# One expert's rows transposed two experts ahead, and the next expert's first products put into the waits of the current one

## The reference, cut to what matters

```python
pg_top, g_sel = lax.top_k(pg, 1)              # one of 4 groups of experts
top_v, top_i = lax.top_k(le_sel, TOP_K)       # 2 of its 8 experts
expert_idx = g_sel * EXPERTS_PER_GROUP + top_i
...
def expert_block(args):
    xe, e = args
    return (jax.nn.silu(xe @ w_gate[e]) * (xe @ w_up[e])) @ w_down[e]
...
x = x + g2 * hier_moe(h, ...)
```

## Time and profile before

| | us |
|---|---|
| three runs: median, lowest, highest | 1513.91, 1513.27, 1514.66 |
| the profiled execution's own time | 1513.77 |
| its span, from the first instruction to the last | 1511.4 |
| PE busy | 1326.7 (88%) |
| DVE busy | 597.8 (40%) |
| ACT busy | 357.1 (24%) |
| POOL busy | 268.0 (18%) |
| mean granted clock of PE, as a share of full speed | 0.958 |

### The profile page before, as it was taken

One profiled execution on the slowest core, in us unless ns is written; L12 is line 12 of the kernel. 1 busy time (PEld: TensorE's weight loads), 2 busy tenths in 40 slices (PEclk: granted clock), 3 DMA queues, 4 the chain that ended last, 5 costly groups with the idle time before them and its releaser, 6 DMA issues.

```text
span 1511.4 us, 18434 instructions
## 1 busy us (share of the span) xinstructions
PE 1326.7 (88%) x6928; PEld 767.9 (51%) x6928; DVE 597.8 (40%) x1314; ACT 357.1 (24%) x791; POOL 268.0 (18%) x283
## 2 busy tenths in 40 slices
PE   5899899988998898888998999999889969997883
PEld 1446546655745554444444565566464545554441
DVE  5635522357716321433154251435782541221112
ACT  1411022545402111111202211244551211111111
POOL 0201200000100353322221030000010015333222
PEclk8999999999999799999987999999999979999997
DMA  8801220555494799999943112135307489999984
GB/s 288 318 16 56 101 84 12 215 191 180 133 361 166 293 327 379 410 404 404 358 170 118 56 58 70 58 133 202 112 1 297 160 299 387 400 400 403 402 343 147
DMA packets 100228, 336.83 MB, mean 223 GB/s; under 512 B 29988, under 2 KB 34724, under 8 KB 74890
## 3 DMA queue, kind: packets, MB, share of 16 engines
q1 hardware_dynamic: 74600, 305.52, 52.1%
q0 software_dynamic: 15072, 16.85, 5.0%
q10 hardware_dynamic: 10468, 13.28, 2.5%
HBM read 324.13 MB, written 29.00 MB: 234 GB/s over the span
## 4 chain that ended last, share of the span: by engine, by line
PE 77%; DVE 12%; ACT 4%; issue 4%; DMA 1%; POOL 1%; SPq 0%; DVEq 0%; POOLq 0%; ACTq 0%
PE bank L504 71%; PE bank L785 3%; PE bank L896 2%; DVE pr_r L2145 2%; ACT pr_r L1502 2%; DVE ht_r L2005 1%; DVE pr_r L2148 1%; PE bank L622 1%; DMA big<-in_ada_w_dram 1%; DVE mix_r L2019 1%; DVE big L1736 1%; DVE small L2003 0%; DMA x_tok<-x_rows 0%; DVE big L1923 0%; DVE ht_r L1989 0%
## 5 line engine op out<-in xcount | busy, mean ns | idle before, releaser
L504 PE MATMUL bank<-big,pr_r 128*64 128x256 f32 (+2 forms) x3032 | 426.3, 400 | 43.8 <-DVE pr_r L2148 22.6
L504 PEld LDWEIGHTS bank<-big,pr_r 128*64 128x64 f32 (+1 forms) x3032 | 258.3, 152 | 181.7 <-issue 93.6
L504 PE MATMUL bank<-big,ht_r 128*128 128x512 f32 (+3 forms) x832 | 309.1, 555 | 1.9 <-ACT ht_r L1455 1.9
L504 PEld LDWEIGHTS bank<-big,ht_r 128*128 128x128 f32 (+1 forms) x832 | 143.5, 189 | 133.0 <-issue 121.5
L504 PE MATMUL bank<-big 128*128 128x256 f32 (+4 forms) x496 | 169.4, 480 | 22.5 <-DVE big L1930 5.9
L1651 POOL DMA_INDIRECT x_rows<-ht_r,slot_i x64 | 102.0, 1594 | 321.4 <-DVE ht_r L2151 302.8
L504 PEld LDWEIGHTS bank<-big 128*128 128x128 f32 (+2 forms) x496 | 92.4, 198 | 67.2 <-issue 29.8
L1502 ACT ACTIVATE pr_r<-bank 64x256 f32<-64x256 f32 x64 | 24.1, 377 | 403.4 <-PE bank L504 403.4
L2145 DVE TENSOR_TENSOR pr_r<-pr_r,bank 64x256 f32<-64x256 f32 x65 | 27.5, 423 | 219.6 <-ACT pr_r L1502 214.6
L2151 DVE SCALAR_TENSOR_TENSOR ht_r<-bank,mix_r,mod 128x512 f32<-128x512 f32 x65 | 48.8, 751 | 132.6 <-PE bank L504 132.6
L504 PE MATMUL bank<-ht_r,big 128*128 128x512 f32 x192 | 85.4, 607 | 1.4 <-ACT ht_r L1341 1.4
(11 more groups left out here) (299 smaller groups left out, 1237.5 us busy)
## 6 DMA issues: line engine op xcount, KB each, us to landing
big<-in_moe_w_gate_dram SPq DMA_DIRECT2D x59, 1024.0 KB, 17.8
big<-in_moe_w_up_dram SPq DMA_DIRECT2D x59, 1024.0 KB, 22.3
big<-in_moe_w_down_dram SPq DMA_DIRECT2D x59, 1024.0 KB, 26.3
big<-in_ada_w_dram SPq DMA_DIRECT2D x16, 3072.0 KB, 11.3
big<-in_w_in_dram SPq DMA_DIRECT2D x4, 3072.0 KB, 13.6
big<-in_w_out_dram SPq DMA_DIRECT2D x4, 2048.0 KB, 9.3
mod<-in_ada_b_dram SPq DMA_DIRECT2D x12, 512.0 KB, 10.4
x_tok<-in_moe_w_gate_dram SPq DMA_DIRECT2D x6, 1024.0 KB, 17.0
```

The costliest lines, as they stand in the source:

```text
L504: return nc.tensor.matmul(o, l, r, start=start, stop=stop)
```

## The change

PE's order becomes, for expert e: gate and up of e, steps 2 to 7; the row transposes of e + 2 (`x_turn`); step 0 of gate and up of e + 1 (`begin`); the activation transposes of e; step 1 of gate and up of e + 1; down of e. The waits go with the work. `x_turn(e + 2)` waits for the gather of e + 2, and `begin(e + 1)` for the weights of e + 1. ACT's copies of the transposed rows follow the new order. The number of matmuls and of transfers is the same, and the programs of POOL, DVE and SP are not edited. There are still four row buffers.

```diff
-                def gate_up(b, s):
+                def gate_up(b, s, ks=range(KT)):
                     wg, wu, _ = expert_slot(s)
-                    for k in range(KT):
+                    for k in ks:
...
-                def expert(e):
-                    b, s = e % 2, EXPERT_SLOTS[l][e]
+                def x_turn(e):
+
+                    pe.wait_ge(gathered[e % 4], NE // 4 * 16 * l + 16 * (e // 4 + 1))
+                    if e >= 2:
+                        pe.wait_ge(xt_ready, NE * l + e - 1)
+                    pe.sem_inc(waited, 1)
+                    x_transpose(e % 2, e % 4).then_inc(xt_done, 1)
+
+                def begin(e):
+
+                    s = EXPERT_SLOTS[l][e]
                     pe.wait_ge(xt_ready, NE * l + e + 1)
                     pe.wait_ge(slot_full[s], expert_full(e, l))
                     if e >= 2:
                         pe.wait_ge(acth_ready, NE * l + e - 1)
-                    gate_up(b, s).then_inc(gu_done, 1)
+                    gate_up(e % 2, s, range(1))
+
+                def expert(e):
+                    b, s = e % 2, EXPERT_SLOTS[l][e]
+                    gate_up(b, s, range(2 if e else 1, KT)).then_inc(gu_done, 1)
                     if e == 0:
...
+                        x_turn(1)
+                    if e + 2 < NE:
+                        x_turn(e + 2)
                     if e + 1 < NE:
-                        pe.wait_ge(gathered[(e + 1) % 4], NE // 4 * 16 * l + 16 * ((e + 1) // 4 + 1))
-                        if e >= 1:
-                            pe.wait_ge(xt_ready, NE * l + e)
-                        pe.sem_inc(waited, 1)
-                        x_transpose(1 - b, (e + 1) % 4).then_inc(xt_done, 1)
+                        begin(e + 1)
                     pe.wait_ge(acth_ready, NE * l + e + 1)
...
                     act_transpose(b).then_inc(at_done, 1)
+                    if e + 1 < NE:
+                        gate_up(1 - b, EXPERT_SLOTS[l][e + 1], range(1, 2))
                     pe.wait_ge(actT_ready, NE * l + e + 1)
...
-                pe.wait_ge(gathered[0], NE // 4 * 16 * l + 16)
-                pe.sem_inc(waited, 1)
-                x_transpose(0, 0).then_inc(xt_done, 1)
+                x_turn(0)
+                begin(0)
                 for e in range(NE):
...
# ScalarE's program
-                    if e + 1 < NE:
-                        act.wait_ge(xt_done, NE * l + e + 2)
-                        x_evac(1 - b).then_inc(xt_ready, 1)
+                    for n in ((1, 2) if e == 0 else (e + 2,)):
+                        if n < NE:
+                            act.wait_ge(xt_done, NE * l + n + 1)
+                            x_evac(n % 2).then_inc(xt_ready, 1)
```

## The result

| | before | after |
|---|---|---|
| runs timed together: median (lowest to highest), us | 1513.59 (1512.09 to 1514.66) | 1566.93 (1563.49 to 1572.23) |
| the profiled execution's own time, us | 1513.77 | 1564.18 |
| its span, us | 1511.4 | 1561.8 |
| mean granted clock of PE | 0.958 | 0.933 |

The ratio is 1.0359, with a 95% interval from 1.0328 to 1.0389: 3.6% slower. Slower was forecast (+18.8 us), but the profiled execution lost 50.4 us, and the time lies outside the range.

The account below looks back on a forecast made before the run. PE's chain of one expert and the stream of weights were both taken as near their limit. Late gathers added 10.8 us in layer 1 and 8.0 in layer 0 to 1513.8: 1532.6 us, range 1520 to 1548.

Parts of the forecast that it names:

- The loop: From one expert's down through POOL's scatter, gather and row transposes to the down two experts later: 16.4 us.
- The free parts: Splitting gate and up costs PE nothing; ACT's changed order lies beside PE's work, else 0.6 us at expert 0.
- The prediction's own sign of being wrong: Wrong if gathers land under 5.5 us, PE waits for weights all through layer 1, or clock share falls well below 0.98.
- D(5) = 1268.5 + 8.8 + 2.1 = 1279.4. Twelve loops of 16.4 give D(29) = 1476.2: In layer 1, expert 5's down starts at 1279.4 us; twelve two-expert turns of 16.4 us bring expert 29's to 1476.2.
- Layer 0: In layer 0, later weight loads plus the moved wait for weights start expert 31's down at 775.1 us, +8.0 us.
- So this adds 5.8 us of dry time: In layer 0, expert 10's loads go out later, with DMA engines already run dry: 5.8 us more dry time.
- The bound of 9: In layer 0, upper bound in us, with slow gathers, on the shift lasting to the end; the lower was 2.
- So the shift stays: After expert 31's down in layer 0, PE goes on into its own long products, so the +8.0 us lasts.
- D: Rival: PE's clock falls in the new waits, 20 us more in layer 1, 1553 us; chance 0.09 in full.
- A: Rival: gathers land in time, under 5.5 us; 1514.5 us, no change; chance 0.06.
- B: Rival: the weight stream has slack too, PE's pace of 6.5 us per expert holds; about 1480 us; chance 0.02.
- C: Gathers near 7.5 us: layer 1 at weights' pace, +2.1; layer 0 +4 to +8; 1520 to 1524 us; chance 0.09.

Follow-up runs that it names:

- the first experiment: Changed kernel, but POOL issues the gather of e + 4 ahead of the scatter of e instead of behind it: 1519.88 us, 1.0054.
- twelve fillers: Changed kernel with twelve 128x128 identity transposes on PE ahead of each wait for a gather, from expert 4 on (layer 0: 4 to 13): 1546.14 us, 1.0198.
- the split: Down weights get their own semaphores, waited for at down: kernel before 1.0004; changed kernel 1.0387, or 1.0000 with the gather issued ahead of the scatter.
- the lighter stream: Changed kernel with half of layer 1's gate and up weights not loaded: 1529.58 us, 1.0093; the kernel before with the same: 1500.39 us, 0.9903.

## Why the prediction was wrong

*The loop was right.* The gather of two experts ahead ends PE's longest waits, the loop is the one described, and the two old waits all but vanish. The free parts were free: with the gather out of the way PE's own period was 6.55 us (the first experiment), 6.5 by forecast. The sum put the fall of the clock in the new waits at nothing, and left it to a rival. The time is off by the length of a turn and by how the turns start. The prediction's own sign of being wrong came true: the clock's share fell to 0.88 in the earlier trace rows's stretch of layer 1.

*The step that failed is "D(5) = 1268.5 + 8.8 + 2.1 = 1279.4. Twelve loops of 16.4 give D(29) = 1476.2".* It took every turn at the full clock and at the median gather of before. The changed kernel, mean of the ten turns from D(5) to D(25) of layer 1, 1297.8 to 1482.8 us, and beside it the same turns with twelve fillers (1294.9 to 1470.0 us; its landings are not in the trace, so its gather is the time from issue to PE's start less 0.13, and at most that, since in two of the ten turns PE came later):

| part of a turn, us | forecast | measured | with twelve fillers |
|---|---|---|---|
| down to the gather's issue | 5.5 | 5.95 | 5.65 |
| gather | 8.8 | 9.56 | 9.51 |
| to PE's start | 0.1 | 0.13 | 0.13 |
| row transposes to the next down | 2.0 | 2.86 | 2.22 |
| sum | 16.4 | 18.5 | 17.5 |

The turns without a fall have 5.5 in the first part and 2.1 in the fourth. So of 2.1 us too few, 1.3 are the clock and 0.8 the gather. The fillers take most of the clock's share away and leave the gather's. Why the gathers took 0.8 us longer than before, no run shows. Ten turns make 21 us. Another 6.5 were there by D(5). Layer 1's first row transposes start 12.0 us late (1240.20 instead of 1228.23), and D(5) is 25.1 us late, so 13.2 in this layer instead of 6.7. In expert 0 the 32 matmuls of gate and up took 6.54 us instead of 5.05 (1.5). The gathers of 4 and 7 took 9.9 and 10.6 us instead of 8.8 (2.9). The clock fell after the wait of 4.58 us ahead of the row transposes of 4 (1.9). From D(25) to D(31) it took 45.5 us, as forecast. So layer 1 added 10.8 + 21 + 6.5 = 38.3 us, and D(31) is 50.3 us late.

*Layer 0* was +8.0 and came out +14.3. "So this adds 5.8 us of dry time" is the term: the loads of expert 10 were 11.2 us late. 1.1 us of it stood in this profile ahead of the first expert; the rest of what was missing is again the gathers of 4 and 6 (10.2 and 9.6 us instead of 8.8) and the clock after the waits of 4.94 and 4.16 us (3.3 and 3.4 us from row transposes to down instead of 2.0). How a late load passes to the end through the full stream was right: 12.0 us later at the last landing, and the tail 7.8 where 7.7 was forecast. The bound of 9 left out that the start could be wrong too. "So the shift stays" did not hold in full: 14.3 us at D(31) were 12.0 at layer 1's first row transposes. Why 2.3 us went in between is open.

*The rivals.* D, the clock, is the one that happened. It had 0.09. I gave it little because one wait of 2.08 us had left the clock alone, though the new waits were to be 3.4 us. Its price of 1.7 us was taken from 32 matmuls; in a turn it is up to 1.3 from row transposes to down (3.4 instead of 2.1) plus up to 1.4 from down to the gather's issue (6.9 instead of 5.5). That rival put its twelve falls at 20 us, the clock's share of the ten turns was 13. A is excluded: the gathers took 9.3 us by the median. B was wrong: with the gather out of the way, PE's faster order brought nothing (1.0054, and 1.0000 with the split). C's term, the moved wait for weights, exists and is 7 to 8 us, but in the changed kernel it does not show beside the gather's loop. By the fit of the Trainium skill ("DMA: Bandwidth & Descriptors", "Anatomy of one DMA — SWDGE (gpsimd) path") an estimate for a gather is 2.6 us. The trace does not agree: the shortest of the changed kernel took 3.3 us, as the stream ran out, and the median in layer 1 was 9.3 us.

*Wait and clock feed each other.* In the turns that start with D(5) to D(9) PE waits twice, mostly 1.4 to 2.2 us each. The clock over such a turn is granted at 0.90 to 1.00, and a turn takes 17.0 to 18.5 us. In those that start with D(13) to D(23) there is one wait of 2.9 to 5.0 us, the clock is at 0.83 to 0.91, and a turn takes 17.5 to 20.5 us. I read it so: once the clock falls, one half of the turn is longer, the waits bunch into one, and that drops the clock again. The runs with fillers fit this, but no run shows the bunching by itself.

## What to carry to other kernels

When work is pulled ahead of a wait, follow its inputs to the engine that issues them and sum the whole loop; then see if that issue really needs what stands ahead of it in its queue: here the order of two calls was worth 46 us. A wait inside a loop on TensorE was to be priced twice here, with the wait and with the work behind it at the lower clock. And where a stream of transfers set the end, no order of PE tried here won more than 0.2%, and those that waited for the weights earlier lost some.

## What the runs showed of the hardware

- Adding work made the kernel faster: 12 transposes of the identity (some 1.5 us) ahead of each wait, 24 us. With them the clock was granted at 1.00 from 1400 to 1490 us, without them at 0.87. Of the two levels, 1.2 and 2.4 GHz, the rows after a long wait show the lower: a step takes 1.12 us instead of 0.65.
- The length of a wait did not settle whether the clock fell: it had after 1.94 and 2.16 us, and had not after 2.00 and 3.06.
- Of the changed kernel's gathers of experts 4 to 31 in layer 1, 26 of 28 took 7.6 to 10.6 us; weights streamed at 366 GB/s from 1240 to 1460 us. Three took 7.0 to 7.8 us in the run with the lighter stream, at a DMA share of 0.71 and 235 GB/s. The changed kernel's two others, and two in layer 0, took 3.3 to 4.3 us as the stream ran out or had run dry.
- With the down weights issued in the same order but counted apart, the up weights landed 6.4 us later in layer 0 while the last transfer landed within 1 us of before: the landing of an early part could not be read off the profile of the other kernel.
